# Latent transposes between the query and key tiles, query rotation in steps, output chunks among the last attention units, rows and row scaling in parts

## Chip, cores and metric

One core of a Trainium2 chip runs the whole program. The metric is device time in microseconds (us): the median of several executions. The engines are named as in the profile: PE (TensorE, matmuls and transposes), PEld (its weight loads), ACT (ScalarE), DVE (VectorE), POOL (GpSimd) and SP (SyncE, which issues the DMAs). Each engine runs its own list of instructions in order, and semaphores join the lists.

## What is computed

Two transformer blocks over 256 tokens of width 2048, all in fp32. The first block is not touched. The second one is:

```python
ada = silu(c) @ w_ada + b_ada                     # six vectors: shift, scale and gate, for mixer and FFN
h = rms_norm(x, g_pre_mix) * (1 + scale_m) + shift_m
c_q, c_kv, k_rope, q_g, k_g, v_g, a_g, r_g = split(h @ w_in)
o_mla = mla(...)    # q from rms_norm(c_q) @ w_uq, k and v from rms_norm(c_kv); 64 of 192 columns are rotated
o_gla = gla(...)    # gated linear attention; log decay = log_sigmoid(a_g @ w_gate_up + b) / 16, chunks of 64
x = x + gate_m * rms_norm(concat(o_mla, o_gla) @ w_out, g_post_mix)
h = rms_norm(x, g_pre_ffn) * (1 + scale_f) + shift_f
x = x + gate_f * rms_norm((silu(h @ w_gate) * (h @ w_up)) @ w_down, g_post_ffn)
```

The latents are c_q (512 columns) and c_kv (256), the gate latent a_g has 16 columns, and the rotated key part 64.

## The kernel before

**Weights.** Every matmul is done in three: both operands are split into a high part (`hi`, rounded to fp32r) and a rest (`lo`), and hi x hi, hi x lo and lo x hi are added in PSUM (`project`, line 597). The weights come as one stream of chunks of 128 x 1024 elements (512 KB) into seven `raw` slots. ACT makes `w_hi` of a chunk (line 1101), DVE `w_lo` (line 1549), into four slots each; both stay up to three chunks ahead of PE (`AHEAD = 3`). A slot is written again when PE is through with the chunk that it held. `round_until(i)` on ACT and `rests_until(i)` on DVE work through the chunks up to number i, and stand between the other instructions of those engines in an order written out by hand. A tile (`tile`) is a product of 128 output columns against 256 tokens and uses one PSUM bank, over 16 pieces of 128 columns for the mixer's input; a group (`group`) is a product of 512 output columns, in a pair of banks. `group_steps` is the same as a generator, which yields after each chunk. A chunk holds eight pieces of a tile or two of a group. The first value piece shares a chunk with the end of the last key tile, and from there on the groups begin in the middle of a chunk, the output projection too.

**Second mixer, order on PE.** Group c_q in banks 0 and 1, group c_kv in 2 and 3; four query tiles and four key tiles (`gla_q`, `gla_k`) in turns on banks 4, 5, 2, 3; then the latents are transposed, one tile k of 128 columns after the other, in banks 6 and 7 in turns (line 881): PE transposes two token halves, ACT rounds the bank into `cq_hi` or `ckv_hi` (line 1326), DVE makes the rest (line 1949), and the bank is free. Behind them come the gate latent (line 886, copied by DVE in line 1951) and the rotated key (line 892). The value and r groups follow, with the gate products (line 902) and the decay work of ACT and DVE between their steps (`decays`). Then q_rope (a group in banks 0 and 1), eight q_nope tiles, the turns of the rotated queries (line 985), eight k_nope tiles and two mla_v groups. Between them the generator `linear` does the linear attention of four heads: turn and score (927, 932), states (942; DVE copies and adds in 2050 and 2054), outputs (949, 955). DVE rotates the queries as one run of twelve operations (`rope`, lines 1958 to 1966).

**Latent units.** 16 units of head and token half: scores (1006, 1007), DVE mask and maximum, ACT exp, DVE weights (2107), transposes two units later (1015), outputs three units later (1025), ACT and DVE round them into `mix_hi` and `mix_lo` (1431, 2113). Then come the four output groups `out2`. Within the first one PE makes the four quarters of the gate as rows, by a matmul of ones with diagonal tiles (`rows`, line 666), which DVE writes (`diagonals`, line 1624) and ACT copies out (line 1451).

**Entry of the FFN.** x is gated and scaled in quarters of 512 columns, by `scale_ffn2(n)` on DVE (lines 2130 and 1564). PE transposes the scaled tiles (line 634, up to three tiles ahead of the product), ACT shifts them (1143), DVE and ACT make `h_hi`, DVE makes `h_lo` (1617). `shift_h` on DVE does this for 16 tiles k; tile k is in quarter k // 4.

Of the kernel before, what the change touches and what calls it, by code (L numbers as in the profile page):

```python
# [6 lines left out]
F32 = mybir.dt.float32  # L7
# [6 lines left out]
P = 128  # L14
T = 256
# [278 lines left out]
def two_blocks(nc, WEIGHTS, X, PARAMS, PARAMS1, PARAMS2, POSITIONS, OUT):  # L294
# [10 lines left out]
    with ctx:  # L305
# [161 lines left out]
        TURN_BANKS = ((6, 7, 0, 1), (6, 7, 0, 1), (6, 7, 4, 5), (6, 7, 4, 5))  # L467
        ROW_BANKS = ((4, 5, 7, 0), (4, 5, 7, 6), (4, 5, 7, 6))
# [82 lines left out]
        def tensor_program(e):  # L551
# [314 lines left out]
            free[2], free[3] = (c_kv_copied, 1), (c_kv_copied, 2)  # L866
            for h in range(GLA_HEADS):
                tile(("gla_q", h), h_hi, h_lo, need, (gla_q_ready, h + 1))
            for h in range(GLA_HEADS):
                tile(("gla_k", h), h_hi, h_lo, need, (gla_k_ready, h + 1))  # L870
            for k in range(KQ + KKV):
                b = 6 + k % 2
                for tt in range(TT):
                    if k < KQ:
                        w.wait_ge(c_q_scaled, tt + 1)
                        src = c_q[:, tt, k * P:(k + 1) * P]
                    else:
                        w.wait_ge(c_kv_scaled, tt + 1)
                        src = c_kv[:, tt, (k - KQ) * P:(k - KQ + 1) * P]
                    fill(b)  # L880
                    t = e.transpose(banks[b][:, tt * P:(tt + 1) * P], src, identity)
                t.then_inc(latent_turned, 1)
                free[b] = latent_ready, k + 1
# [5 lines left out]
            for tt in range(TT):  # L889
                w.wait_ge(k_rotated, tt + 1)  # L890
                fill(7)
                t = e.transpose(banks[7][:, tt * P:(tt + 1) * P], k_rot[:, tt, :, :].rearrange("p a c -> p (a c)"), identity)
            t.then_inc(k_rot_turned, 1)
            free[7] = k_rope_ready, 1
# [13 lines left out]
            for at_group, key in enumerate((("gla_v", 0), ("gla_v", 1), ("gla_r", 0), ("gla_r", 1))):  # L908
                pair = (2 * (at_group % 2), 2 * (at_group % 2) + 1)
                for _ in group_steps(key, 512, pair, h_hi, h_lo, need):  # L910
                    if at_group < 3:
                        next(decaying, None)
                if at_group == 2:
                    whole(decaying)
# [113 lines left out]

            for u in range(NM + 3):
# [7 lines left out]
            whole(linear)  # L1037

            tiles["of"], tiles["turn"] = (4, 5, 2, 3), 0
            mix2_need = lambda k: w.wait_ge(mla_ready, 2 * k + 2) if k < KD // 2 else w.wait_ge(gla_ready, k - KD // 2 + 1)  # L1040
# [48 lines left out]
        def scalar_program(e):  # L1089
# [224 lines left out]
            e.activation(sine, angle, ACT.Sin).then_inc(rope_ready, 1)  # L1314
            for h in range(GLA_HEADS):
                out = made(("gla_q", h))
                e.activation(gla_q[:, h, :], out[:, 0:T], ACT.Copy, scale=float(np.float32(GLA_K ** -0.5))).then_inc(gla_q_ready, 1)
            for h in range(GLA_HEADS):
                out = made(("gla_k", h))
                e.activation(gla_k[:, h, :], out[:, 0:T], ACT.Copy).then_inc(gla_k_ready, 1)  # L1320
            w.wait_ge(row_made, 4)
            for k in range(KQ + KKV):
                w.wait_ge(latent_turned, k + 1)
                dst = cq_hi[:, k, :] if k < KQ else ckv_hi[:, k - KQ, :]
                gain = param("g_q")[:, k:k + 1] if k < KQ else param("g_kv")[:, k - KQ:k - KQ + 1]
# [1130 lines left out]
```

## Time and profile before

| | |
|---|---|
| runs | 2352.96, 2351.81, 2357.68 us; median 2352.96 |
| profiled execution | 2351.76 us, of which the span of the trace 2350.0 |
| mean granted clock of PE | 0.984 |
| PE busy | 2268.7 us, 97% |
| DVE busy | 1590.2 us, 68% |
| ACT busy | 1086.1 us, 46% |
| chain that ended last | PE 86%, DVE 8%, ACT 2% |
| HBM read | 494.38 MB |

A row of the time line gives start and length in us, engine, line, operation, output and inputs, and in square brackets how long the engine had been idle before it and what ended that. Matmuls are pipelined: each starts before the one ahead of it has ended, so pace is read from start to start.

### The profile page before, as it was taken

To read this page: it belongs to the slowest core of one execution; us is meant where nothing else is said; L and a number is where in the kernel's file an instruction comes from. 1 tells how busy PE (TensorE), PEld (TensorE's weight loads), DVE (VectorE), ACT (ScalarE), POOL (GpSimd) and SP (SyncE) were. 2 spreads that over 40 slices of the span, in tenths; PEclk is the share of its full clock that TensorE was granted. 3 is DMA by queue.
4 is the path that set the end of the run, shared out by engine and by line. 5 is a ranking of instruction groups with operands and counts; after the bars stand their busy time and mean duration, and the time that the engine had idled before them with its cause. 6 is when DMAs were issued, how large, how long until landed. Compare 5 with 4: busy or idle time off the path is not lost.

```text
span 2350.0 us, 33555 instructions
## 1 busy us (share of the span) xinstructions
PE 2268.7 (97%) x13738; PEld 1993.7 (85%) x13738; DVE 1590.2 (68%) x2203; ACT 1086.1 (46%) x1601; POOL 19.3 (1%) x44
## 2 busy tenths in 40 slices
PE   7999999999999999999999999998999999999997
PEld 7999777999998899998879776677888988888886
DVE  6898785788887688888775564547555555554554
ACT  5333774544443344444454564445444344444442
POOL 0000000000000000000000001000000000000000
PEclk9999999999999999999999999999999999999999
DMA  8753436688888788888856451355666677655553
GB/s 240 262 171 126 146 95 207 202 279 277 286 293 310 280 286 276 280 279 291 291 186 196 152 179 55 103 170 190 225 231 231 207 234 232 224 181 187 188 184 110
DMA packets 137897, 501.82 MB, mean 214 GB/s; under 512 B 15328, under 2 KB 15456, under 8 KB 137488
## 3 DMA queue, kind: packets, MB, share of 16 engines
q1 hardware_dynamic: 136512, 494.44, 62.3%
q0 software_dynamic: 1232, 5.24, 1.4%
q8 instruction: 108, 1.77, 0.3%
q14 instruction: 45, 0.37, 0.0%
HBM read 494.38 MB, written 5.24 MB: 213 GB/s over the span
## 4 chain that ended last, share of the span: by engine, by line
PE 86%; DVE 8%; ACT 2%; DMA 1%; issue 1%; POOL 0%; SPq 0%; DVEq 0%; ACTq 0%
PE bank L597 54%; PE both L597 26%; DVE w_lo L1549 3%; DVE conv_y L1655 2%; DMA raw<-weights 1%; PE bank L566 1%; ACT w_hi L1101 1%; PE bank L797 1%; PE both L758 1%; PE bank L779 0%; PE bank L666 0%; PE bank L1060 0%; PE bank L634 0%; ACT junk L1114 0%; DMA x<-x 0%
## 5 line engine op out<-in xcount | busy, mean ns | idle before, releaser
L1549 DVE TENSOR_TENSOR w_lo<-raw,w_hi 128x1024 fp32r<-128x1024 f32 x737 | 889.9, 1220 | 477.8 <-ACT w_hi L1101 476.8
L1101 ACT ACTIVATE w_hi<-raw 128x1024 fp32r<-128x1024 f32 x737 | 763.5, 1054 | 664.2 <-PE bank L597 383.6
L597 PE MATMUL bank<-h_hi,w_hi 128*128 128x256 f32 (+1 forms) x2064 | 595.1, 288 | 12.5 <-DVE w_lo L1549 11.9
L597 PE MATMUL bank<-h_lo,w_hi 128*128 128x256 f32 (+1 forms) x2064 | 588.2, 285 | 0.0
L597 PE MATMUL bank<-h_hi,w_lo 128*128 128x256 f32 (+1 forms) x2064 | 587.9, 285 | 0.0
L597 PEld LDWEIGHTS bank<-h_hi,w_hi 128*128 128x128 f32 (+1 forms) x2064 | 399.3, 193 | 19.9 <-DVE w_lo L1549 17.4
L597 PEld LDWEIGHTS bank<-h_lo,w_hi 128*128 128x128 f32 (+1 forms) x2064 | 399.4, 194 | 0.1
L597 PEld LDWEIGHTS bank<-h_hi,w_lo 128*128 128x128 f32 (+1 forms) x2064 | 399.3, 193 | 0.0
L1533 DVE SCALAR_TENSOR_TENSOR ada_acc<-raw,stat,ada_acc 128x1024 f32<-128x1024 f32 x180 | 230.1, 1278 | 0.0
L597 PE MATMUL bank<-w_hi,h_hi 128*128 128x512 f32 (+2 forms) x512 | 190.7, 373 | 0.0
L597 PE MATMUL bank<-w_hi,h_lo 128*128 128x512 f32 (+2 forms) x512 | 190.1, 371 | 0.0
L597 PE MATMUL bank<-w_lo,h_hi 128*128 128x512 f32 (+2 forms) x512 | 190.1, 371 | 0.0
L597 PE MATMUL both<-w_hi,h_hi 128*128 128x512 f32 (+1 forms) x480 | 186.1, 388 | 3.1 <-DVE h_lo L1617 2.5
L597 PE MATMUL both<-w_hi,h_lo 128*128 128x512 f32 (+1 forms) x480 | 181.9, 379 | 0.0
L597 PE MATMUL both<-w_lo,h_hi 128*128 128x512 f32 (+1 forms) x480 | 181.9, 379 | 0.0
L597 PE MATMUL bank<-w_hi,ff_hi 128*128 128x512 f32 x352 | 138.6, 394 | 1.8 <-DVE w_lo L1549 1.8
L597 PE MATMUL both<-w_hi,ff_hi 128*128 128x512 f32 x352 | 138.2, 393 | 0.6 <-DVE w_lo L1549 0.6
L597 PE MATMUL bank<-w_hi,ff_lo 128*128 128x512 f32 x352 | 137.0, 389 | 0.0
L597 PE MATMUL both<-w_hi,ff_lo 128*128 128x512 f32 x352 | 137.0, 389 | 0.0
L597 PE MATMUL both<-w_lo,ff_hi 128*128 128x512 f32 x352 | 137.0, 389 | 0.0
L597 PE MATMUL bank<-w_lo,ff_hi 128*128 128x512 f32 x352 | 136.9, 389 | 0.0
L597 PEld LDWEIGHTS bank<-w_hi,h_hi 128*128 128x128 f32 x512 | 96.4, 188 | 17.1 <-issue 0.7
(352 smaller groups left out, 2711.9 us busy)
## 6 DMA issues: line engine op xcount, KB each, us to landing
raw<-weights SPq DMA_DIRECT2D x924, 512.0 KB, 4.4
bias_rows<-table POOLq DMA_DIRECT2D x1, 3072.0 KB, 35.1
raw<-weights SPq DMA_DIRECT2D x5, 504.0 KB, 3.8
x<-x SPq DMA_DIRECT2D x2, 1024.0 KB, 5.8
bias<-bias_rows POOLq DMA_DIRECT2D x1, 2048.0 KB, 17.0
out<-x SPq DMA_DIRECT2D x8, 256.0 KB, 2.2
phase<-params SPq DMA_DIRECT2D x1, 497.0 KB, 10.5
raw<-weights SPq DMA_DIRECT2D x1, 488.0 KB, 3.3
```

The lines of the kernel that those rows point to most:

```text
L566: t = e.matmul(banks[6][:, k:k + 1], ada_acc[:, sums[0] % 2, k * P:(k + 1) * P], ones[:, 0:1], start=True, stop=True)
L597: t = e.matmul(out, s, m, start=opens and first and q == 0, stop=closes and last and q == 2)
L758: t = e.matmul(both[:, side, br * n:(br + 1) * n], queries[r, j, tt * P:(tt + 1) * P], keys[r, br, j // GQA, 0:n], start=True, stop=True)
L797: t = e.matmul(banks[b][DH * side:DH * side + DH, 0:P], values[:, sb, br, hk * DH:(hk + 1) * DH], weights_T[v % 2][:, (2 * side + br) * (t ...
L1101: e.activation(w_hi[:, n % PART_SLOTS, 0:widths[i]], raw[:, i % RAW_SLOTS, 0:widths[i]], ACT.Copy).then_inc(hi_ready, 1)
L1533: e.scalar_tensor_tensor(acc, src, s, acc, ALU.mult, ALU.add).then_inc(ada_summed, 1)
L1549: e.tensor_tensor(w_lo[:, slot, 0:widths[i]], raw[:, i % RAW_SLOTS, 0:widths[i]], w_hi[:, slot, 0:widths[i]].bitcast(F32), ALU.subtract).t ...
L1655: t = e.scalar_tensor_tensor(y, u, tap_w, y, ALU.mult, ALU.add)
```

## The change

On PE the latent transposes are put into three places: k = 0 and 1 behind the fourth query tile (banks 6, 7), k = 2 and 3 behind the first key tile (banks 0, 1), k = 4 and 5 behind the second (banks 6, 7). ACT and DVE round them at the same places of their lists. The gate latent stays behind the last key tile; DVE does the key rotation before its copy, and PE transposes the rotated key behind the third step of the first value group. The query rotation becomes a generator, of which DVE does one of eight steps at each q_nope tile. During the mla_v groups DVE goes three chunks ahead. The first three steps of the first output group are done in the last three rounds of the latent units, and the rows in two parts, in the first and the second output group. At the entry of the FFN the quarters are scaled at k = 1, 4 and 8 instead of before k = 0, at 2 and at 6.

```diff
+        LATENT_BANKS = (6, 7, 0, 1, 6, 7)
+        WITH_GLA_Q = ((), (), (), (0, 1))
+        WITH_GLA_K = ((2, 3), (4, 5), (), ())
...
+            def turn_latents(ks):
+                for k in ks:
+                    b = LATENT_BANKS[k]
...
+                    t.then_inc(latent_turned, 1)
+                    free[b] = latent_ready, k + 1
...
             for h in range(GLA_HEADS):
                 tile(("gla_q", h), h_hi, h_lo, need, (gla_q_ready, h + 1))
+                turn_latents(WITH_GLA_Q[h])
             for h in range(GLA_HEADS):
                 tile(("gla_k", h), h_hi, h_lo, need, (gla_k_ready, h + 1))
-            for k in range(KQ + KKV):
-                b = 6 + k % 2
...
+                turn_latents(WITH_GLA_K[h])
...
+            def turn_k_rope():
+                for tt in range(TT):
+                    w.wait_ge(k_rotated, tt + 1)
...
+                    if at_group == 0 and at_step == 2:
+                        turn_k_rope()
...
+            first_out = group_steps(("out2", 0), 512, (0, 1), mix_hi, mix_lo, mix2_need)
             for u in range(NM + 3):
...
-            whole(linear)
+                if u == NM - 1:
+                    whole(linear)
+                if u >= NM:
+                    next(first_out)
...
-                steps = group_steps(("out2", n), 512, pair, mix_hi, mix_lo, mix2_need)
-                if n == 0:
-                    for quarters in ((0, 1), (2, 3)):
-                        next(steps)
-                        rows(4, quarters)
+                steps = group_steps(("out2", n), 512, pair, mix_hi, mix_lo, mix2_need) if n else first_out
+                if n < 2:
+                    next(steps)
+                    next(steps)
+                    rows(4, ((0, 1), (2, 3))[n])
...
             def shift_h(stage, scale):
                 scale(0)
-                scale(1)
+                if stage == 2:
+                    scale(1)
                 for k in range(KD):
-                    if k in (2, 6):
+                    if stage == 2 and k in (2, 6):
                         scale(2 + k // 4)
+                    if stage == 3 and k in (1, 4, 8):
+                        scale(1 + k // 4)
...
-            rests_until(final["gla_k", GLA_HEADS - 1] + AHEAD)
-            for k in range(KQ + KKV):
...
+            for h in range(GLA_HEADS):
+                rests_until(final["gla_q", h] + AHEAD)
+                rest_latents(WITH_GLA_Q[h])
+            for h in range(GLA_HEADS):
+                rests_until(final["gla_k", h] + AHEAD)
+                rest_latents(WITH_GLA_K[h])
...
+            for _ in rotate_keys():
+                pass
+            w.wait_ge(a_lr_turned, 1)
+            e.tensor_copy(a_lr[:, :], banks[6][0:GATE_RANK, 0:T]).then_inc(a_lr_ready, 1)
...
+                    if at_group == 0 and piece == 7:
+                        place_k_rope()
...
+            rotating = rotate_queries()
             for h in range(MLA_HEADS):
                 rests_until(final["q_nope", h] + AHEAD)
+                next(rotating, None)
                 if h % 2:
                     next(linear)
...
             for n in range(2):
-                rests_until(ada_first - 1)
+                rests_until(final["mla_v", n] + AHEAD)
                 next(linear)
...
             for n in range(4):
+                rests_until(min(final["out2", n] + AHEAD, gate_first - 1))
                 if n == 0:
-                    rests_until(groups["out2", 0][3][0] + AHEAD)
                     diagonals(4, ada(2), (2, 3))
-                rests_until(min(final["out2", n] + AHEAD, gate_first - 1))
```

`turn_latents` has the body of the loop that it replaces, as have `round_latents` on ACT and `rest_latents` on DVE. `rope` yields after its first pair of products, after the difference, after its second pair and after the sum. ACT copies the rows of the gate two by two, in the first and second output group.

## Rows read from the trace of the kernel before

**Rows 1.** The page, part 1: busy time, share and instructions.
```profile
PE 2268.7 (97%) x13738; PEld 1993.7 (85%) x13738; DVE 1590.2 (68%) x2203; ACT 1086.1 (46%) x1601; POOL 19.3 (1%) x44
```

**Rows 2.** PE's waits from 1198 to 1625: total us, times, longest us.
```profile
PE bank L942 <- DVE g_state L2050: 6.1, 4, 3.8
PE bank L666 <- DVE diag L1624: 3.2, 1, 3.2
PE bank L892 <- DVE k_rot L1974: 2.4, 2, 1.7
```

**Rows 3.** Stretches: length, busy us by engine (count), PEclk, DMA share, GB/s.
```profile
1410.05:1416.80 6.75, 6.69 (x27) 6.05 (x28) 2.18 (x4) 1.35 (x3) 0.00 (x0) 0.50 0.26 80
1426.00:1431.00 5.00, 3.60 (x25) 2.43 (x22) 2.14 (x4) 1.69 (x6) 0.00 (x0) 1.00 0.34 118
1450.00:1454.30 4.30, 3.49 (x16) 2.06 (x16) 3.76 (x12) 2.66 (x6) 0.09 (x1) 1.00 0.00 0
1454.40:1457.75 3.35, 3.35 (x9) 1.42 (x8) 1.00 (x4) 0.75 (x3) 0.13 (x1) 0.50 0.00 0
1485.15:1488.45 3.30, 2.89 (x9) 2.53 (x10) 1.58 (x8) 0.28 (x1) 0.00 (x0) 0.50 0.00 0
```

**Rows 4.** Time line of PE from the first latent transpose to the value group.
```profile
1295.97 0.60 PE L881 MATMUL bank<-lasting,c_q 128*128 128x128 f32 x4
...
1307.52 0.72 PE L902 MATMUL bank<-a_lr,phase 16*128 16x256 f32 x2
...
1308.74 0.40 PE L597 MATMUL both<-w_hi,h_lo 128*128 128x512 f32 x1
1308.97 0.40 PE L597 MATMUL both<-w_hi,h_hi 128*128 128x512 f32 x1
```

**Rows 5.** Time line of DVE in the same stretch.
```profile
1296.25 1.23 DVE L1549 TENSOR_TENSOR w_lo<-raw,w_hi 128x1024 fp32r<-128x1024 f32 x1 [1.65 <-ACT w_hi L1101]
...
1301.66 0.41 DVE L1951 COPY a_lr<-bank 16x256 f32<-16x256 f32 x1 [0.29 <-PE bank L886]
...
1304.30 0.20 DVE L1974 COPY k_rot<-k_rot 128x64 f32<-128x64 f32 x1
```

**Rows 6.** Time line of PE around the first head's states.
```profile
1405.60 0.70 PE L942 MATMUL bank<-gla_v,g_kdn 64*128 64x256 f32 x4
1410.11 1.22 PE L942 MATMUL bank<-gla_v,g_kdn 64*128 64x256 f32 x2 [3.80 <-DVE g_state L2050]
...
1416.54 0.74 PE L949 MATMUL bank<-gla_v,g_at 128*128 128x256 f32 x2
```

**Rows 7.** Time line of ACT and DVE around the query rotation.
```profile
1404.56 1.05 ACT L1101 ACTIVATE w_hi<-raw 128x1024 fp32r<-128x1024 f32 x1
...
1408.04 0.42 DVE L1966 TENSOR_TENSOR q_rot<-rope_tmp 128x256 f32<-128x256 f32 x1
1408.49 1.23 DVE L1549 TENSOR_TENSOR w_lo<-raw,w_hi 128x1024 fp32r<-128x1024 f32 x1
```

**Rows 8.** Time line of PE, last latent units and rows.
```profile
1484.29 0.49 PE L1025 MATMUL bank<-m_T,mla_v 128*128 128x128 f32 x2 [0.34 <-DVE mix_lo L2113]
1485.56 1.19 PE L1025 MATMUL bank<-m_T,mla_v 128*128 128x128 f32 x4 [0.78 <-DVE mix_lo L2113]
...
1496.72 1.98 PE L666 MATMUL bank<-diag,lasting 128*128 128x512 f32 x4 [3.25 <-DVE diag L1624]
```

**Rows 9.** Time line of DVE behind the last latent unit.
```profile
1487.42 1.66 DVE L1624 TENSOR_SCALAR diag<-lasting 128x128 f32<-128x128 f32 x8
```

**Rows 10.** Time line of PE, first and ninth tile of the FFN's h.
```profile
1594.00 0.80 PE L597 MATMUL both<-w_hi,h_hi 128*128 128x512 f32 x1 [2.28 <-DVE h_lo L1617]
...
1609.03 0.47 PE L597 MATMUL both<-w_hi,h_hi 128*128 128x512 f32 x1 [0.18 <-DVE w_lo L1549]
```

**Rows 11.** Time line of DVE, its only idle time from 1589.6 to 1608.
```profile
1606.71 0.43 DVE L1617 TENSOR_TENSOR h_lo<-work,h_hi 128x256 fp32r<-128x256 f32 x1 [0.22 <-ACT h_hi L1146]
1607.66 1.22 DVE L1549 TENSOR_TENSOR w_lo<-raw,w_hi 128x1024 fp32r<-128x1024 f32 x1 [0.52 <-ACT w_hi L1101]
```

More of the change, by code:

```diff
@@ L888, in tensor_program @@
             free[6] = a_lr_ready, 1
[L889 to L894, printed above, removed]
+            def turn_k_rope():
+                for tt in range(TT):
+                    w.wait_ge(k_rotated, tt + 1)
+                    fill(7)
+                    t = e.transpose(banks[7][:, tt * P:(tt + 1) * P], k_rot[:, tt, :, :].rearrange("p a c -> p (a c)"), identity)
+                t.then_inc(k_rot_turned, 1)
+                free[7] = k_rope_ready, 1
             def decays():
@@ L909, in tensor_program @@
                 pair = (2 * (at_group % 2), 2 * (at_group % 2) + 1)
-                for _ in group_steps(key, 512, pair, h_hi, h_lo, need):
+                for at_step, _ in enumerate(group_steps(key, 512, pair, h_hi, h_lo, need)):
                     if at_group < 3:
                         next(decaying, None)
+                    if at_group == 0 and at_step == 2:
+                        turn_k_rope()
                 if at_group == 2:
@@ L1314, in scalar_program, with round_latents @@
             e.activation(sine, angle, ACT.Sin).then_inc(rope_ready, 1)
+            def round_latents(ks):
+                for k in ks:
+                    w.wait_ge(latent_turned, k + 1)
+                    dst = cq_hi[:, k, :] if k < KQ else ckv_hi[:, k - KQ, :]
+                    gain = param("g_q")[:, k:k + 1] if k < KQ else param("g_kv")[:, k - KQ:k - KQ + 1]
+                    e.activation(dst, banks[LATENT_BANKS[k]][:, 0:T], ACT.Copy, scale=gain).then_inc(latent_rounded, 1)
+            w.wait_ge(row_made, 4)
             for h in range(GLA_HEADS):
@@ L1447, in scalar_program @@
                 outs = made(("out2", n))
-                if n == 0:
-                    for q in range(4):
+                if n < 2:
+                    for q in (2 * n, 2 * n + 1):
                         w.wait_ge(row_made, 4 + q + 1)
@@ L1964, in rope, with rotate_keys, place_k_rope @@
                 t = chain(e.tensor_tensor(tb, src1, sin_b, ALU.mult))
+                yield
                 w.wait_ge(dve_step, t)
[L1966 to L1977 removed]
+                if done_sem is None:
+                    chain(e.tensor_tensor(dst2, ta, tb, ALU.add))
+                else:
+                    e.tensor_tensor(dst2, ta, tb, ALU.add).then_inc(done_sem, 1)
+                yield
+            def rotate_keys():
+                tmp_k = rope_w[:, 4, :, :]
+                for tt in range(TT):
+                    k1 = c_kv[:, tt, KV_RANK:KV_RANK + ROPE2].unsqueeze(1)
+                    k2 = c_kv[:, tt, KV_RANK + ROPE2:KV_RANK + ROPE].unsqueeze(1)
+                    yield from rope(k1, k2, k_rot[:, tt, 0:1, 0:ROPE2], k_rot[:, tt, 0:1, ROPE2:ROPE], 1, tt, tmp_k[:, 0:1, :], tmp_k[:, 1:2, :], None)
+                    w.wait_ge(dve_step, step[0])
+                    e.tensor_copy(k_rot[:, tt, 1, :], k_rot[:, tt, 0, :]).then_inc(k_rotated, 1)
+            for _ in rotate_keys():
+                pass
+            w.wait_ge(a_lr_turned, 1)
+            e.tensor_copy(a_lr[:, :], banks[6][0:GATE_RANK, 0:T]).then_inc(a_lr_ready, 1)
+            def place_k_rope():
+                w.wait_ge(k_rot_turned, 1)
+                w.wait_ge(latent_squares, 2 * TT)
+                e.tensor_copy(k_rope_x[:, :], banks[7][:, 0:T]).then_inc(k_rope_ready, 1)
             keep = param2("chunk_causal").bitcast(I32)
```

71 lines of the change are left out of this document (29 added, 42 removed).

## The prediction

> **What bounds the kernel now.** I read the page first: TensorE is busy for 97% of the span, VectorE for 68% and ScalarE for 46% [rows 1], and no wait of TensorE in the stretch of the change leads to a transfer; TensorE sets the pace as a whole. Only two things can then be won: time in which TensorE waits, and time in which it runs at half of its clock. So I read, second, the waits of TensorE in the second mixer and at the entry of its FFN, which is all that the diff touches [rows 2]: 6.1 us on the state copies (3.8 of them at one place), 3.2 on a diagonal, 2.4 on the rotated keys. Third, the granted clock of the stretches behind those waits [rows 3]: 0.50, the 1.2 GHz level, from 1410.05 to 1416.80, from 1454.40 to 1457.75 and from 1485.15 to 1488.45, and 1.00, the 2.4 GHz level, in the others. A stretch at 0.50 costs half of its length. Last, the order of time around each place, for the instruction that a wait hangs on. Everything below counts instants of TensorE, because its work itself (the same matmuls and transposes) is unchanged.
>
> **A. Latent turns.** Before, the twelve turns of the latents, two of the gate latent and two of the rotated key come in one block behind the last key tile, and each pair of turns waits for ScalarE and VectorE to empty its bank. From the first turn to the first gate product 11.55 us pass, 1295.97 to 1307.52 [rows 4]. Afterwards twelve turns stand in three groups of four behind a tile whose bank is another. Their inputs are scaled by VectorE right behind the latent groups, several tiles earlier, and four banks make them free of the round trip. Four turns end 0.60 after their start [rows 4]; the next matmul starts before that end, so I take 0.5 for a group, 1.5 for three (bounds 1.2 and 1.8). ScalarE and VectorE keep three weight chunks ahead, each worth 24 matmuls of 256 columns or 12 of 512, that is 12 x 0.23 = 2.8 us [rows 4]; 8 us of cover hide their two roundings per latent.
>
> What is late next is the gate latent. VectorE now does, in its own order, the low part of the last chunk ahead, then the whole key rotation, and only then the copy that the first gate product waits for. The low part started at 1296.25 and takes 1.23; shifted by 1.5 it ends at 1299.0. The key rotation took from 1302.07 (end of the copy) to 1304.50, 2.4 us; the copy takes 0.41 [rows 5]. So the copy ends at 1301.8. TensorE is there at 1295.97 + 1.5 + 0.3 (two gate turns) + 1.4 (six matmuls at 0.23) = 1299.2 and waits 2.6 us. That is a wait that this change makes: queued behind it on TensorE are all value matmuls, whose operands are ready. The stretch becomes 5.8 instead of 11.55; the two key turns, moved into the value group, add 0.3. Gain 5.4 (bounds: 3.7 if the clock falls for one stretch of 3.3 as in [rows 3]; 8.0 if the rotation were hidden). The wait on the rotated keys itself goes: they are ready long before step 2, and the copy of the turned key on VectorE has four chunks before bank 7 is wanted.
>
> **B. Query rotation in steps.** Before, VectorE rotates all queries in one go and then does a low part (1408.49, 1.23) before the state copy; TensorE stands 3.80 us, resumes at 1410.11, 0.39 behind that low part, and works at half clock until 1416.54 [rows 6, 7, 3]. Afterwards, when the first state product comes at 1405.60, VectorE has done one step and waits for the high part that ends at 1404.56 + 1.05 = 1405.61; then low part 1.23, one operation of the rotation 0.42, copy 0.4: 1407.65 [rows 7]. TensorE wins 2.45 us of wait. The 6.43 us from 1410.11 to 1416.54 hold two state matmuls and 24 of 256 columns, which take about 3.5 at full clock (0.6 and 24 x 0.12, half of the pace of 512 columns): 2.9 more. The eighth step stands ahead of the next head's state copy and adds its 0.4. The rotated queries are complete by then, so their turns wait for nothing new. Gain 4.9 (bounds 2.1, if the clock falls all the same, and 5.4).
>
> **C. Low parts earlier.** Two low parts that came after the latent units now stand among the value matmuls, ahead of a state copy; that copy can be 0 to 1.23 late. VectorE mostly waits there, so I take 0.3 lost. This is the price of the cover in D.
>
> **D. End of the latent units and rows.** TensorE waits 0.34 and 0.78 for the last units, then runs its first output matmuls at 0.50 up to 1488.45, then waits 3.25 for the third diagonal [rows 8, 3]. VectorE made the first two diagonals in 1.66 [rows 9]; the third is late because it stands behind the low part of a chunk that needs TensorE's own progress. Afterwards output chunks of 6, 12 and 12 matmuls stand between the last units: 1.4 and 2.8 us of work over waits of 0.34 and 0.78, which go (1.1). The engine then is dense, so the low stretch goes (half of 3.3: 1.65). The third diagonal is wanted in the second output group, 18 matmuls (4 us) after the end of the first, while it is made about 2 us after that end; the 3.25 go, and ScalarE's four row copies are halved between two groups. Could the fifth chunk be late, since ScalarE rounds it only after the last unit? Two chunks, 5.5 us, cover what stands before it, about 3 (the last rounding of the mix, a high part of 1.05 and a low part of 1.23 [rows 7]). Gain 6.0 (bounds 3.3, the diagonal alone, and 6.3).
>
> **E. Scaling order at the FFN.** The scaling of the second quarter moves behind the first tile of h: TensorE's wait of 2.28 ends some 2.1 us sooner [rows 10], when ScalarE has shifted the first tile. But VectorE's list up to the low part at 1607.66 is the same list in another order, and it was idle for only 0.22 and 0.52 on the way [rows 11]. TensorE needed it at 1609.03 [rows 10]. So 2.1 won at the start shrink to 0.7 at the ninth tile (bounds 0 and 2.1).
>
> **Sum.** 5.4 + 4.9 - 0.3 + 6.0 + 0.7 = 16.7 us, against the profiled execution's own 2351.8 (span 2350.0 and 1.8 around it): 2335.1. The median of the runs stands 1.2 above that execution, so I forecast 2336.
>
> **A rule weighed.** Row first: with TensorE busy for 3.60 of 5.00 us from 1426 the clock stayed at 1.00, and with 3.49 of 4.30 busy from 1450 it fell to 0.50 at 1454.40 [rows 3]; short waits alone do not tell. The Trainium skill, page "TensorE: Matmul & The Clock Gate", section "A second HAM failure mode: psum-queue depth-cycling", says that small idle times between groups of matmuls that cycle through banks make the clock swing between its levels. That speaks against this change, which puts many small groups between tiles; by it the gains of clock in A, B and D would be in doubt, and the sum nearer to the second rival below. The row of 1454.40 agrees with it, that of 1426 does not.
>
> **Rivals.** First, the waits shrink less: the low part and the step do not fit before the state product, and quarter scaling gives nothing (E 0, B 2.5): 16.7 - 2.4 - 0.7 = 13.6, 2339.4. It blends with the second. Second, the clock falls at the new small waits: at A's 2.6, at B's 1.35 and once among the last units, each time for 3.3 us, half lost: 16.7 - 5.0 = 11.7, 2341. For it: the fall at 1454.40 with hardly any wait. Against it: all three stand beside dense matmuls of 256 and 512 columns, whereas the known falls came behind 3.8 us of rest or among small matmuls. Third, the gate wait of A is hidden after all and the FFN keeps its 2.1: 20.7, 2332. Fourth, no change to measure: the gains must shrink below 7, for instance if the state copies, the diagonal and the quarter each pass their wait to the next chunk. Against it: at each place the chunks that follow are rounded three ahead, so an instant won is kept, but for E. Fifth, slower: the turns between tiles stall ScalarE, which stands in order before the latent's bank while its weight chunks fall due. It decides once a group is late by more than the cover of 8 us; to lose 16.7 and 7 more it would need 24 us, 8 beyond the cover at each of three groups, 2360 or more. The whole block before, with every round trip and the key rotation in it, took 11.55 [rows 4], less than half of that.
>
> **Numbers.** Forecast (2333.5 to 2339) 0.58; first rival 0.13; second 0.12 (together 2339 to 2345); third 0.08; none 0.06; slower 0.03. A measurement of this kernel tells changes from none at about 0.3%, 7 us: faster 0.91, same 0.06, slower 0.03. Range 2331 to 2344: the first three cases but for their tails.
>
> **What would show it.** A: transposes behind the fourth query tile and the first two key tiles without a wait, and one wait of 2 to 3 us of the gate product on the copy of the gate latent. B: the longest wait on the state copy under 1.6, and clock 1.00 behind it. C: a state wait longer by 0.3 near the value matmuls. D: no wait on a diagonal, none on the mix behind the last score. E: the first FFN matmul 2 us nearer to its turns, but a wait on a low part around the ninth tile. The forecast is wrong if the gate product waits 5 us or more, if new stretches at 0.50 appear, or if a wait on low parts shows in the first output group.

## The result and the profile after

The changed kernel takes 2334.43 us (median of 4 runs, 2334.12 to 2334.65); the kernel before, run again beside it, takes 2355.07 (4 runs, 2351.81 to 2357.68). The ratio is 0.9915, with a 95% interval from 0.99 to 0.9931: faster, by 0.7 to 1.0%. The forecast was 2336, with a range from 2331 to 2344. The profiled execution took 2334.39 with a span of 2332.6, at a mean granted clock of 0.988, where the one of before took 2351.76. From here on a low stretch is one at a granted clock of 0.50, and a turn is a transpose on TensorE. The page, part 1, shows the same instructions as [rows 1] and 6.3 us less of TensorE's busy time, since fewer of them ran at half clock (in the first block too):

```profile
PE 2262.4 (97%) x13738; PEld 1989.3 (85%) x13738; DVE 1589.2 (68%) x2203; ACT 1085.5 (47%) x1601; POOL 19.2 (1%) x44
```

The waits of TensorE from 1198 to 1625 answer to [rows 2]: total us, times, longest us.

```profile
PE bank L637 <- DVE wide L1583: 12.4, 2, 7.9
PE bank L953 <- DVE g_state L2094: 4.2, 4, 1.3
PE bank L911 <- DVE a_lr L2014: 2.5, 1, 2.5
PE both L600 <- DVE h_lo L1639: 1.3, 3, 0.8
PE both L600 <- DVE w_lo L1568: 1.3, 3, 0.9
```

The wait on a diagonal and the one on the rotated key are gone, that on the state copies went from 6.1 to 4.2, and the gate latent has a new one of 2.5. (The line numbers of the changed kernel are a little higher: its matmul is L600, its states L953, its low parts of the weights L1568.)

Now the places one by one. TensorE at the gate product, then VectorE around the copy that it waits for, as in [rows 4, 5]:

```profile
1276.77 0.60 PE L881 MATMUL both<-lasting,c_q 128*128 128x128 f32 x4
...
1299.20 0.69 PE L911 MATMUL bank<-a_lr,phase 16*128 16x256 f32 x2 [2.52 <-DVE a_lr L2014]
```
```profile
1295.18 1.23 DVE L1568 TENSOR_TENSOR w_lo<-raw,w_hi 128x1024 fp32r<-128x1024 f32 x1 [1.65 <-ACT w_hi L1116]
1296.33 0.18 DVE L1985 TENSOR_TENSOR rope_w<-c_kv,rope_w 128x32 f32<-128x32 f32 x1
...
1298.63 0.19 DVE L2009 COPY k_rot<-k_rot 128x64 f32<-128x64 f32 x1
1298.74 0.41 DVE L2014 COPY a_lr<-bank 16x256 f32<-16x256 f32 x1
```

The turns wait for nothing (a row without square brackets), and the copy stands behind the whole key rotation, 2.4 us from 1296.33 to 1298.74. The first head's states on TensorE, and VectorE beside them, as in [rows 6, 7]:

```profile
1397.55 0.70 PE L953 MATMUL bank<-gla_v,g_kdn 64*128 64x256 f32 x4
1399.53 0.70 PE L953 MATMUL bank<-gla_v,g_kdn 64*128 64x256 f32 x2 [1.28 <-DVE g_state L2094]
...
1404.63 0.60 PE L960 MATMUL bank<-gla_v,g_at 128*128 128x256 f32 x2
```
```profile
1397.58 1.22 DVE L1568 TENSOR_TENSOR w_lo<-raw,w_hi 128x1024 fp32r<-128x1024 f32 x1 [1.40 <-ACT w_hi L1116]
1398.73 0.42 DVE L1989 TENSOR_TENSOR q_rot<-rope_tmp 128x256 f32<-128x256 f32 x1
1399.06 0.42 DVE L2094 COPY g_state<-bank 128x256 f32<-128x256 f32 x1
```

The wait is 1.28 where the forecast had 1.35, and for the forecast's reason: low part, one step, copy. But the stretches (length, busy us by engine with counts, PEclk, DMA share, GB/s) show what [rows 3] showed before, shorter:

```profile
1400.55:1403.90 3.35, 3.35 (x18) 3.35 (x18) 0.86 (x3) 1.09 (x2) 0.00 (x0) 0.50 0.34 136
1404.00:1409.00 5.00, 5.00 (x34) 3.57 (x33) 2.57 (x5) 1.79 (x8) 1.48 (x4) 1.00 0.30 105
1417.65:1421.00 3.35, 3.18 (x16) 3.02 (x15) 0.00 (x0) 1.01 (x4) 0.00 (x0) 0.50 0.03 11
1444.95:1448.30 3.35, 3.35 (x10) 1.09 (x8) 1.08 (x4) 0.61 (x3) 0.74 (x2) 0.50 0.00 0
1468.00:1476.00 8.00, 7.09 (x40) 5.36 (x40) 5.00 (x19) 4.33 (x16) 0.00 (x0) 1.00 0.00 0
```

Behind the state wait of the first head and behind that of the second (1415.53, also 1.28) TensorE runs at 0.50, the 1.2 GHz level, among matmuls that the forecast had at 1.00. Behind the second it ran at 1.00 before [rows 3], so that low stretch is new. The end of the latent units is at 1.00, as forecast. TensorE there and at both row groups, as in [rows 8]:

```profile
1475.10 0.48 PE L600 MATMUL both<-w_hi,mix_hi 128*128 128x512 f32 x1
...
1477.96 0.60 PE L1036 MATMUL bank<-m_T,mla_v 128*128 128x128 f32 x4
...
1486.58 1.88 PE L669 MATMUL bank<-diag,lasting 128*128 128x512 f32 x4
...
1501.94 1.88 PE L669 MATMUL bank<-diag,lasting 128*128 128x512 f32 x4
```

No row has a wait. The FFN's first, fifth and ninth tile, as in [rows 10]:

```profile
1575.31 0.80 PE L600 MATMUL both<-w_hi,h_hi 128*128 128x512 f32 x1 [0.24 <-DVE h_lo L1639]
...
1584.06 0.50 PE L600 MATMUL both<-w_hi,h_hi 128*128 128x512 f32 x1 [0.82 <-DVE h_lo L1639]
...
1591.66 0.47 PE L600 MATMUL both<-w_hi,h_hi 128*128 128x512 f32 x1 [0.88 <-DVE w_lo L1568]
```

2.04 are won at the first tile and 0.72 are left at the ninth, the rest being given back in the waits of 0.82 and 0.88 (before, 0 and 0.18).

From start to start of the same instruction of TensorE in both traces, the difference of the spans goes to these stretches (us, minus is shorter):

| stretch | measured | forecast |
|---|---|---|
| first block and up to the first query tile (start 1249.56, then 1247.21), which the change does not touch | -2.35 | 0 |
| A: to the gate product -5.97; value group with the key turns +0.25 | -5.7 | -5.4 |
| B: first head's states to its outputs -3.86, next stretch -0.13; second head's states to its outputs +1.61 | -2.4 | -4.9 |
| C: third head's states (wait 0.51, then 0.81) | +0.3 | +0.3 |
| D: last score to second output group -8.33; rows moved into that group +1.76 | -6.6 | -6.0 |
| E: first FFN tile -2.04, up to the ninth +1.32 | -0.7 | -0.7 |

In the changed stretch 15.1 against 16.7 forecast. What remained to be settled: whether the parts are independent, whether the clock in B belongs to the waits, whether C is the cover of D, and how much of the total is chance.

### The profile page after: what moved, and what is told of

It reads as the page before. It is cut to its first block, busy times and chain, and to the rows that moved or that the text cites. A ratio compares the mean times of both kernels' runs of the same rounds, so it can differ in the third digit from the quotient of the medians.

```text
span 2332.6 us, 33553 instructions
## 1 busy us (share of the span) xinstructions
PE 2262.4 (97%) x13738; PEld 1989.3 (85%) x13738; DVE 1589.2 (68%) x2203; ACT 1085.5 (47%) x1601; POOL 19.2 (1%) x44
## 4 chain that ended last, share of the span: by engine, by line
PE 86%; DVE 8%; ACT 2%; DMA 1%; issue 1%; POOL 0%; SPq 0%; DVEq 0%; ACTq 0%
PE bank L600 54%; PE both L600 26%; DVE w_lo L1568 3%; DVE conv_y L1677 2%; DMA raw<-weights 1%; PE bank L569 1%; ACT w_hi L1116 1%; PE bank L800 1%; PE both L761 1%; PE bank L782 1%; PE bank L637 0%; PE bank L1075 0%; ACT junk L1129 0%; PE bank L669 0%; DVE x L2181 0%
## 5 line engine op out<-in xcount | busy, mean ns | idle before, releaser
L1568 DVE TENSOR_TENSOR w_lo<-raw,w_hi 128x1024 fp32r<-128x1024 f32 x737 | 889.9, 1220 | 473.4 <-ACT w_hi L1116 471.9
L600 PE MATMUL bank<-h_hi,w_hi 128*128 128x256 f32 (+1 forms) x2064 | 594.8, 288 | 10.8 <-DVE w_lo L1568 10.1
L600 PE MATMUL bank<-h_lo,w_hi 128*128 128x256 f32 (+1 forms) x2064 | 586.9, 284 | 0.0
L600 PE MATMUL bank<-h_hi,w_lo 128*128 128x256 f32 (+1 forms) x2064 | 586.8, 284 | 0.0
L600 PEld LDWEIGHTS bank<-h_hi,w_hi 128*128 128x128 f32 (+1 forms) x2064 | 397.9, 193 | 19.0 <-DVE w_lo L1568 16.7
L600 PEld LDWEIGHTS bank<-h_lo,w_hi 128*128 128x128 f32 (+1 forms) x2064 | 398.3, 193 | 0.1
L600 PEld LDWEIGHTS bank<-h_hi,w_lo 128*128 128x128 f32 (+1 forms) x2064 | 398.0, 193 | 0.0
L600 PE MATMUL bank<-w_hi,h_hi 128*128 128x512 f32 (+2 forms) x512 | 190.7, 373 | 0.0
L600 PE MATMUL bank<-w_hi,h_lo 128*128 128x512 f32 (+2 forms) x512 | 190.1, 371 | 0.0
L600 PE MATMUL bank<-w_lo,h_hi 128*128 128x512 f32 (+2 forms) x512 | 190.1, 371 | 0.0
L600 PE MATMUL both<-w_hi,h_hi 128*128 128x512 f32 (+1 forms) x480 | 185.4, 386 | 2.6 <-DVE h_lo L1639 1.3
L600 PE MATMUL both<-w_hi,h_lo 128*128 128x512 f32 (+1 forms) x480 | 181.4, 378 | 0.0
L600 PE MATMUL both<-w_lo,h_hi 128*128 128x512 f32 (+1 forms) x480 | 181.1, 377 | 0.0
L600 PE MATMUL bank<-w_hi,ff_hi 128*128 128x512 f32 x352 | 139.3, 396 | 1.8 <-DVE w_lo L1568 1.8
L600 PE MATMUL both<-w_hi,ff_hi 128*128 128x512 f32 x352 | 138.2, 393 | 0.6 <-DVE w_lo L1568 0.6
L600 PE MATMUL bank<-w_lo,ff_hi 128*128 128x512 f32 x352 | 137.7, 391 | 0.0
L600 PE MATMUL bank<-w_hi,ff_lo 128*128 128x512 f32 x352 | 137.6, 391 | 0.0
L600 PE MATMUL both<-w_hi,ff_lo 128*128 128x512 f32 x352 | 137.0, 389 | 0.0
L600 PE MATMUL both<-w_lo,ff_hi 128*128 128x512 f32 x352 | 137.0, 389 | 0.0
L600 PEld LDWEIGHTS bank<-w_hi,h_hi 128*128 128x128 f32 x512 | 96.4, 188 | 17.1 <-issue 0.7
```

Of the source, the lines that this page charges most:

```text
L600: t = e.matmul(out, s, m, start=opens and first and q == 0, stop=closes and last and q == 2)
L1568: e.tensor_tensor(w_lo[:, slot, 0:widths[i]], raw[:, i % RAW_SLOTS, 0:widths[i]], w_hi[:, slot, 0:widths[i]].bitcast(F32), ALU.subtract).t ...
```

## Experiments

Each kernel was timed beside the kernel before. The median of that one was 2355.08 (2349.56 to 2359.6) in the first four, 2356.82 (2348.22 to 2360.5) in the next four and 2355.77 (2347.52 to 2359.36) in the last four.

| kernel | median (lowest to highest) | ratio, 95% interval | span of the profiled execution |
|---|---|---|---|
| A alone | 2348.08 (2343.47 to 2348.89) | 0.9968, 0.9956 to 0.9981 | 2345.4 |
| B alone | 2349.54 (2347.22 to 2353.21) | 0.998, 0.9968 to 0.9992 | 2345.6 |
| C and D alone | 2346.13 (2344.41 to 2348.51) | 0.9968, 0.9955 to 0.998 | 2343.9 |
| E alone | 2354.45 (2346.7 to 2356.71) | 0.9993, 0.998 to 1.0006 | 2354.6 |
| gate first | 2332.03 (2330.65 to 2334.61) | 0.9902, 0.9884 to 0.9921 | 2332.8 |
| states first | 2335.77 (2334.3 to 2337.64) | 0.9916, 0.9898 to 0.9935 | 2334.9 |
| gate and states | 2330.79 (2330.16 to 2332.3) | 0.9896, 0.9878 to 0.9914 | 2329.0 |
| without C | 2339.34 (2338.37 to 2342.97) | 0.9934, 0.9917 to 0.9951 | 2337.0 |
| rows in parts only | 2338.08 (2335.84 to 2340.74) | 0.9925, 0.9909 to 0.9941 | 2339.0 |
| chunks among units only | 2341.74 (2339.3 to 2344.41) | 0.9944, 0.9929 to 0.9959 | 2342.6 |
| changed kernel again | 2336.21 (2334.09 to 2338.93) | 0.9919, 0.9904 to 0.9934 | 2337.1 |
| all three edits | 2329.59 (2328.14 to 2331.95) | 0.9892, 0.9875 to 0.991 | 2330.2 |

### One part at a time

Four kernels made from the one before, each with one part of the change (C goes with D). Their edits are hunks of the diff shown above; these lines mark A (with its counterparts on ACT and DVE), B, C, D and E in turn:

```diff
+                turn_latents(WITH_GLA_Q[h])
+                next(rotating, None)
+                rests_until(final["mla_v", n] + AHEAD)
+                    next(first_out)
+                    if stage == 3 and k in (1, 4, 8):
```

A alone. 

> Part A alone on the kernel before (latent turns in three groups on four banks, key rotation ahead of the gate copy, key turn in the value group). Additive theory, from the two traces: the gate product comes 6.0 us earlier and q_rope starts 5.7 earlier, with one wait of about 2.5 us of the gate product on the copy of the gate latent, so 5.7 us faster as a whole. Rival (the parts help each other through the clock): under 4 us, with a stretch at 0.50 behind the gate product's wait.

B alone. 

> Part B alone (query rotation in eight steps among the q_nope tiles). Additive theory: 3.9 us won behind the first head's states and 1.5 lost behind the second head's, 2.4 net, with waits of 1.3 us at both state products and a stretch at 0.50 behind each. Rival (the falls of the clock in the changed kernel are a matter of where its stretches happened to lie): the first one stays at 1.00 and the net is 4 to 5 us, as the prediction had it.

C and D alone. 

> Parts C and D alone (low parts three chunks ahead in the value matmuls, output chunks in the last latent rounds, rows in two parts). Additive theory: 0.3 lost at the third head's states and 6.6 won from the last units to the end of the second output group, 6.2 faster, no wait on a diagonal. Rival (the diagonal's wait alone counts, the rest is taken back by the rounding of the fifth chunk): 3.3.

E alone. 

> Part E alone (quarters of the FFN's entry scaled at k = 1, 4, 8). Theory: VectorE's list bounds the stretch, so 2.0 us won at the first tile and 0.7 left from the ninth on, with waits of 0.8 at the fifth tile on its rest and 0.9 at the ninth on a low part: 0.7 faster, which the timing cannot tell from nothing. Rival (TensorE bounds it, as the wait before suggested): 2 us.

By stretch, each part does what it does in the whole. A: -5.96 and +0.25, with the new wait of 2.52. C and D: +0.35 at the third head, then -8.36 and +1.76. E: -2.04 at the first tile and -0.71 left at the ninth. B: from the first head's states to its outputs -5.35, the forecast's 2.45 + 2.9 (measured 2.52 of wait and 2.83 of clock), where the full change had -3.86; at the second head's states +1.46. The net is 3.9, between the 2.4 and the 4 to 5 of the two theories: the first low stretch stayed away, the second did not. The wait at the first head is the same 1.28 in both. In B alone the clock stayed up behind it:

```profile
1403.92 0.70 PE L942 MATMUL bank<-gla_v,g_kdn 64*128 64x256 f32 x2 [1.28 <-DVE g_state L2058]
```
```profile
1404.80:1408.00 3.20, 3.20 (x26) 2.92 (x25) 1.35 (x4) 1.60 (x3) 0.00 (x0) 1.00 0.41 155
```

The times are noisier than the stretches: the medians give 7.0 for A, 5.5 for B, 9.0 for C and D, 0.6 for E, together 22.1, against 20.6 for the whole; the interval of each ratio is about 3 us wide to either side, so the two sums can't be told apart. The stretches show where some of the noise lies. In E alone TensorE ran at 0.50 for 13.6 us among the latent units, which E does not touch (+3.9 there); in the trace of the kernel before it did so for 3.35 [rows 3].

```profile
1452.65:1466.25 13.60, 13.60 (x38) 7.56 (x38) 5.80 (x19) 4.64 (x17) 1.48 (x4) 0.50 0.01 2
```

Around the diagonals of the first output group E alone lost about another 3.0, also at 0.50 and also in a place that E does not touch.

### The new wait of the gate latent

```diff
-            for _ in rotate_keys():
-                pass
             w.wait_ge(a_lr_turned, 1)
             e.tensor_copy(a_lr[:, :], banks[6][0:GATE_RANK, 0:T]).then_inc(a_lr_ready, 1)
+            for _ in rotate_keys():
+                pass
```

> The changed kernel, but VectorE copies the gate latent before the rotation of the key. If the 2.5 us that the first gate product waits are the price of the order on VectorE (the rotation stands before the copy), the wait goes, the stretch from the c_q group to the gate product is 2.4 shorter and the time is about 2332 us. The rival: the rotation now stands before the next low part instead, a weight chunk of the first value group is late by as much, and the time stays at 2334. A third way: the clock of TensorE falls somewhere in the second mixer where it did not, which gives back 1.7 for each stretch of 3.4 at 0.50.

The wait is gone (TensorE at the gate product, no brackets) and the stretch up to it is 8.39 shorter than before instead of 5.97: 2.42, as expected. No wait on a low part came in its place.

```profile
1301.07 0.48 PE L911 MATMUL bank<-a_lr,phase 16*128 16x256 f32 x1
```

No low stretch stands behind the first head's states either (1.5 less). The median is 2332.03, also as expected. The profiled execution was the slowest of the five (2334.61): it reached the mixer 4.2 us later than the trace of the changed kernel did.

### The state waits

```diff
             for h in range(MLA_HEADS):
+                if h in (1, 7):
+                    next(linear)
                 rests_until(final["q_nope", h] + AHEAD)
                 next(rotating, None)
-                if h % 2:
+                if h in (3, 5):
                     next(linear)
```

> The changed kernel, but before the state products of the first and the last head VectorE makes the state copies before the low part of the next chunk and before its step of the query rotation. If the waits of 1.28 us are what brings the clock to 0.50 behind them (1400.5 and 1417.6), both waits shrink to 0.2 or less and both low stretches go: 2.2 + 2 x 1.7 = 5.6 less, about 2329 us. The rival: the clock falls there by itself, among matmuls that use half of the array or few columns, whatever the wait; then only the waits are won, 2.2, about 2332. If the low part that is put behind the copies is wanted at once, a wait on it takes their place and nothing is won.

The expectation calls the states at h = 7 those of the last head; they are those of the second of four, behind the last query tile. Both state waits fall from 1.28 to 0.51, not to the 0.2 expected. The stretch of the first head is 6.12 shorter than before, with the clock at 1.00: the low stretch is gone. That of the second head is 3.74 longer than before: the eighth step of the rotation now stands behind the state copy, the turns of the rotated queries wait for it, and the low stretch there is 6.8 us long instead of 3.4. Neither theory had this wait:

```profile
1415.26 0.70 PE L953 MATMUL bank<-gla_v,g_kdn 64*128 64x256 f32 x2 [0.51 <-DVE g_state L2094]
...
1418.00 2.28 PE L996 MATMUL bank<-lasting,q_rot 128*128 128x128 f32 x8 [2.04 <-DVE q_rot L1999]
```

So the median, 2335.77, is not below that of the changed kernel (2334.43 and 2336.21): the edit was wrong in its second half, and its time alone says nothing on the clock. The two edits together:

> Both edits together: the gate latent copied before the key rotation, and the state copies before the low part and the rotation step. If the two are independent, the gains add up: between 4.6 (waits only, 2330 us) and 8.0 (with both low stretches, 2326 us). The rival: the earlier arrival moves later stretches to other instants and the clock falls there, so that the sum is short by 1.7 for each stretch of 3.4.

The median is 2330.79, just above the 2326 to 2330 expected, with the same wait of 2.04 and a low stretch of 3.4 behind it; behind the first head's states the clock is at 1.00. The last kernel moves the rotation one tile earlier, so that it ends before the second head's state copy:

```diff
                 rests_until(final["q_nope", h] + AHEAD)
+                if h == 4:
+                    next(rotating)
                 next(rotating, None)
```

> The kernel with the gate latent copied before the key rotation and the state copies before the low part, and with two steps of the query rotation instead of one at the fifth q_nope tile, so that the rotation is complete one tile earlier. If the 2.0 us that the turns of the rotated queries wait in the run with both edits are nothing but the last step pushed behind the state copy, they go, and with them most of the 1.7 of the low stretch behind: 2327 to 2329 us. The rival: the clock falls in that place in any case (it did in every run so far, with a wait ahead of it or not), then only the 2.0 are won, 2329; or the doubled step makes the low part at the sixth tile late and a wait of 0.4 to 0.8 shows there.

The wait of 2.04 is gone, and so is the low stretch behind the second head's states. TensorE at both states, and the stretches behind them:

```profile
1400.78 0.70 PE L953 MATMUL bank<-gla_v,g_kdn 64*128 64x256 f32 x2 [0.51 <-DVE g_state L2094]
...
1414.51 0.70 PE L953 MATMUL bank<-gla_v,g_kdn 64*128 64x256 f32 x2 [0.51 <-DVE g_state L2094]
```
```profile
1401.40:1404.30 2.90, 2.90 (x25) 2.90 (x25) 2.71 (x5) 1.17 (x2) 0.00 (x0) 1.00 0.17 17
1416.00:1420.00 4.00, 3.76 (x28) 3.42 (x29) 0.86 (x1) 2.65 (x7) 0.00 (x0) 1.00 0.36 131
1442.95:1446.30 3.35, 3.35 (x9) 1.18 (x10) 0.83 (x2) 0.55 (x3) 0.74 (x2) 0.51 0.00 0
```

B is then worth 6.13 + 0.13 + 0.44 = 6.7, and the whole 2329.59, a little above the 2327 to 2329 expected: 4.8 and 6.6 below the two medians of the changed kernel. It is the lowest median here, though its four runs (2328.14 to 2331.95) overlap those of "gate and states". The rival that the clock falls behind the second head's states in any case is out, since here it did not; whether the shorter wait keeps it up each time, one trace can't show. The low stretch among the latent units stayed.

### C as the cover of D

```diff
             for n in range(2):
-                rests_until(final["mla_v", n] + AHEAD)
+                rests_until(ada_first - 1)
                 next(linear)
```

> The changed kernel without its part C: during the two mla_v groups VectorE makes only the low parts that it made before, and the next two are left for the time behind the latent units. By the prediction C costs 0.3 at a state copy and is the cover for the output chunks among the last units: without it the second or third output chunk waits for its low part, 1.2 to 2.5 us, and the time is 2335 to 2337. The rival: VectorE has room for both low parts among the units' own work, no wait on a low part shows, and the time is 0.3 better or the same.

The third head's state wait is back at 0.51 (0.3 won), and a chunk of the output projection waits for its low part, behind which the clock is near 0.5:

```profile
1481.12 0.50 PE L600 MATMUL both<-w_hi,mix_hi 128*128 128x512 f32 x1 [3.52 <-DVE w_lo L1568]
```
```profile
1481.95:1485.30 3.35, 3.35 (x10) 2.63 (x9) 2.52 (x3) 0.00 (x0) 0.00 (x0) 0.53 0.96 287
```

From the last score to the second output group 5.4 are lost, 3.5 of them in the wait and most of the rest at the half clock behind it. The direction is that of the forecast, the size is more than its 1.2 to 2.5: the low parts stand behind two diagonals (1.66, from 1478.28), which the expectation forgot, and the clock fell behind the wait. The median is 2339.34, above the 2335 to 2337 expected, and 3.1 to 4.9 above those of the changed kernel. So 0.3 spent at a state copy buys 3.5 of wait here, and 5.4 with the clock.

### The two halves of D

Rows in parts, but no output chunk among the last units:

```diff
                     whole(linear)
-                if u >= NM:
-                    next(first_out)
```

> The changed kernel without output chunks among the last three latent units: the rows stay in two parts, the third diagonal belongs to the second output group. By the prediction the chunks among the units are worth 1.1 of waits for the mix and 1.65 of a low stretch, so 2.75 come back, 2337 us, and no wait on a diagonal shows. The rival: the chunks only fill waits that the engine then has elsewhere, nothing comes back, 2334.5.

Output chunks among the last units, but all rows in the first output group (shown on PE and for the diagonals on DVE; ACT's copies of the rows follow):

```diff
-                if n < 2:
-                    next(steps)
-                    next(steps)
-                    rows(4, ((0, 1), (2, 3))[n])
+                if n == 0:
+                    for quarters in ((0, 1), (2, 3)):
+                        next(steps)
+                        rows(4, quarters)
...
-                rests_until(min(final["out2", n] + AHEAD, gate_first - 1))
                 if n == 0:
+                    rests_until(groups["out2", 0][9][0] + AHEAD)
                     diagonals(4, ada(2), (2, 3))
+                rests_until(min(final["out2", n] + AHEAD, gate_first - 1))
```

> The changed kernel with the output chunks among the last units, but with all four quarters of the rows in the first output group, behind its fourth and fifth step. By the prediction the third diagonal stands behind the low part of a chunk that TensorE's own progress releases, so its wait of 3.25 comes back whole or nearly, about 2337.5 us. The rival: with three chunks done among the units VectorE is past that low part in time, the wait is below 1 and the time 2334.5 to 2335.

TensorE's waits of the first kernel from 1470 to 1520, then of the second from 1470 to 1500:

```profile
PE bank L1036 <- DVE mix_lo L2162: 1.1, 2, 0.8
```
```profile
PE bank L669 <- DVE diag L1646: 3.3, 1, 3.3
```

With the rows in parts alone, D gives -5.03 + 1.76 = -3.3, the diagonal to the tenth; the chunks are worth 3.3 on top, against 1.1 + 1.65 expected. With the chunks alone the diagonal's wait is back whole, 3.25, the clock is at 0.51 for 3.3 us behind it, and D gives only 1.45. The halves alone make 4.7, together 6.6: the low stretch behind the diagonal takes about what is missing (half of 3.3). In the trace of before no such stretch follows the diagonal, but in those of A, B and E alone, where the wait is also 3.25, one does; so D would be worth more against a run of the old kernel that has it. Both medians (2338.08, 2341.74) lie above the expectations of 2337 and 2337.5.

### The changed kernel once more

> The changed kernel once more, without an edit. If the low stretch at 1400.5 belongs to the wait of 1.28 ahead of it, it stands there again, and the time is 2334.4 within 0.3. If it is a matter of the run, it is absent in some, and the waits stay as they were to 0.1 us: 2332.5 to 2336.

The times lie between 2334.09 and 2338.93, the median is 2336.21, just above the second theory's 2332.5 to 2336. The profiled execution is the slowest. Its waits at the gate product and the states are those of the first trace to 0.01 us, but its clock fell at other places. TensorE at the gate product and at the first head's states, and the stretches behind them:

```profile
1302.68 1.22 PE L911 MATMUL bank<-a_lr,phase 16*128 16x256 f32 x2 [2.52 <-DVE a_lr L2014]
...
1405.92 0.70 PE L953 MATMUL bank<-gla_v,g_kdn 64*128 64x256 f32 x2 [1.28 <-DVE g_state L2094]
```
```profile
1301.95:1308.70 6.75, 6.02 (x14) 4.30 (x15) 3.08 (x7) 0.00 (x0) 0.00 (x0) 0.51 0.40 135
1406.80:1409.50 2.70, 2.70 (x24) 2.70 (x24) 1.00 (x3) 1.22 (x2) 0.00 (x0) 1.00 0.44 170
1421.45:1428.20 6.75, 6.45 (x31) 5.81 (x30) 0.94 (x2) 3.48 (x8) 0.00 (x0) 0.51 0.15 58
```

Behind the gate wait the half clock cost 2.9 more here, behind the first head's state wait it cost nothing, and behind the second head's the low stretch is twice as long. So the low stretch of 1400.55 does not follow from the wait of 1.28.

## Why the prediction was right, and where not

**What bounds it.** TensorE's waits and its time at half clock were the only thing to win; the instruction counts are the same, and a wait that was won shows in the time unless another took its place, as in E and in "states first".

**A** was right in mechanism and size: no wait at the turns, a new one of 2.52 (2.6 forecast) behind the key rotation, 5.7 won instead of 5.4. The third rival, that the gate wait is hidden, is out: it stood in every trace with that order, and "gate first" took it away for 2.4. What the text did not say is that its 11.55 us held a low stretch, which [rows 3] lacks (kernel before):

```profile
1300.80:1307.55 6.75, 4.07 (x11) 2.25 (x11) 3.55 (x18) 0.02 (x1) 0.00 (x0) 0.50 0.00 0
```

TensorE works 4.07 us in it, so about 2 of A's 5.7 are clock. The waits of the old block were 5.3 together (1.35, 0.78, 0.76, 1.72, 0.73) against the 2.52 of now, which gives 2.8. In the repeated run, where a low stretch of 6.8 stands at the gate product, A is worth only 2.8, below its lower bound of 3.7.

**B** is the step that was mis-sized: 4.9 forecast, 2.4 in the trace of the changed kernel. Its waits were right (2.45 forecast, 2.52 won). The term that failed is the clock, "2.9 more" with 1.00 behind the shorter wait: 1.5 of the 2.9 were lost again behind the first head's states, and 1.3 more behind the second head's, for which the forecast had only the 0.4 of the step. This is the second rival, at one of its three places (B's 1.35), and at one it had not named (the second head's states). At A's wait it came true only in the trace of the repeated run. B alone and "gate first" show the 2.9 as forecast, so the term was not impossible but a matter of the run; in the one trace of "all three edits", with both waits at 0.51, both low stretches are absent. By the prediction's own sign, "new stretches at 0.50 appear", the forecast fails in B: the stretch of 1417.65 is new. The sum held because the other parts and the front made up for it.

**C** and **E** were right to a tenth. E's reason too: the same list in another order gives an early start, and the gain shrinks as the list catches up. C's cover is worth 5.4, against 1.2 to 2.5 expected before that run.

**D** was right in both mechanisms, 6.6 against 6.0 and a little above its upper bound of 6.3. The bound of 3.3, the diagonal alone, is what the rows in parts give by themselves. The fifth chunk was not late, so the fall-back that the text weighed did not come.

**The sum.** 16.7 forecast, 15.1 measured in the changed stretch; the 2.35 at the front, where both kernels have the same instructions, made up for it: that is luck. The median of the kernel before over more runs is 2355 to 2357, 3 to 5 above its profiled execution and not the 1.2 that the forecast added, and that of the changed kernel 2334.4 and 2336.2. So the forecast of 2336 rests in part on errors that cancel. The fourth rival (none) and the fifth (slower) had no sign: ScalarE and VectorE kept their chunks ahead at the turns.

**The rule weighed.** By the row of 1444.95 TensorE fell to 0.50 among the short products of the latent units, where it waits for hardly anything, and a stretch of that kind stands there in all kernels that have the whole change or an edit of it but the repeated run. The Trainium skill, page "TensorE: Matmul & The Clock Gate", section "A second HAM failure mode: psum-queue depth-cycling", says that small idle times between groups of matmuls that cycle through PSUM banks can make the clock swing. This trace agrees in so far as the clock falls among such groups, 1.9 us behind a wait of 0.81 at 1442.99, in a place that the change leaves as it was; no run here varied the cycling. The new small groups of A (turns of four between tiles) show no low stretch in any of the ten traces that have them, which the rule would have let one fear.

What stays open: why the clock fell behind the same wait of 1.28 in some runs and not in others, and why the units' low stretch took 3.4 us in ten traces, 6.8 and 13.6 in one each (both with the mixer's front as before) and none in two. No experiment here controlled that.

## What to carry to other kernels

When TensorE sets the pace, price a shortened wait in two terms, the wait itself and the clock behind it, and give the second a range of its own: in the changed kernel the first came out to 0.1 us (2.52 for 2.6, 1.28 for 1.35), while the low stretch behind the same wait was there in one trace and not in the next. An instruction that another engine waits for belongs ahead of housekeeping of its own engine (a low part for a chunk three ahead, a rotation wanted later); but look what that housekeeping's last piece is wanted for, since the reordered piece becomes the next wait (2.04 here). And a part of a change that costs a little by itself may be the cover of another: 0.3 for 5.4, 3.5 of it wait.

## What the runs showed of the hardware

**The same wait, different clocks.** The waits at the gate product, the states, the diagonal and the scaled tiles (2.52, 0.51, 0.81, 1.28, 3.25, 7.85) repeat to 0.02 us from trace to trace, the granted clock behind them does not. Of the traces in which the first head's states wait 1.28, four have a low stretch behind it (the changed kernel, without C, and both halves of D) and three do not (B alone, gate first, the repeated run): 1.5 us between them. Behind the second head's states with 1.28 there is one in all seven, 3.4 long in six of them and 6.8 in the repeated run; the turns of the rotated queries, small transposes that wait 0.26 for a bank, follow it. Behind the longer wait of the gate product, 2.52 before dense matmuls of 512 columns, there is one in one trace of seven. Of the five traces in which the diagonal waits 3.25, four have a low stretch that ends 3.3 to 5.8 us behind the end of that wait (A, B and E alone, chunks only); the kernel before has none. So the length of the wait alone does not tell. In the three traces in which the first head's states wait 0.51 there is none.

**Scatter of a whole kernel.** The kernel before, with its waits of 3.80 and 3.25, ranged over 13 us in 55 runs (2347.52 to 2360.5; over 10.0 to 12.3 within the 29, 11 and 11 runs beside the experiments), the changed one over 4.8 in 10 runs and the one with all three edits over 3.8 in 4. E alone ranged over 10.0 in 10 runs, A, B and C with D alone over 4.1 to 6.0 in 8 to 10. The removed waits took low stretches with them, and with those perhaps part of the difference from run to run; only the profiled executions show the stretches, so this is not shown. The first block alone, the same in all of them, brings TensorE to the first product of the second mixer between 1204.4 and 1210.5.
